# Value products of three attentions: two exponentials subtracted before one product, and fp16 pairs in place of fp32

## The reference, cut to what matters

```
# first block, 4 heads of width 128, each with two softmaxes over all keys (and 16 meta keys)
attn = softmax(q1 k1' * scale + bias) - lam * softmax(q2 k2' * scale + bias);   y = attn @ v
# (beside it a windowed attention, 8 heads of width 64, which the change leaves alone)
# second block, layer 0: 8 heads of width 64, dense and causal
y = softmax(causal(q k' * scale)) @ v
# second block, layer 1: 16 heads in 4 groups; per head three parts, each with a gate
y = g0 * softmax(q kc') @ vc + g1 * softmax(q ks') @ vs + g2 * softmax(q kw') @ vw
```

## Time and profile before

| what | us |
|---|---|
| median of 3 runs | 2100.46 (2099.26 to 2101.49) |
| the profiled execution | 2099.9 |
| its span, first to last instruction | 2098.1 |
| TensorE busy | 2036.8 (97%) |
| VectorE busy | 1185.9 (57%) |
| ScalarE busy | 809.9 (39%) |
| GpSimd busy | 38.5 (2%) |

### The profile page before, as it was taken

The page is one execution under the profiler, slowest core; times in us unless marked ns, Lnnn a source line. Parts: engine busy times, 40 slices in busy tenths (PEclk is TensorE's granted clock), DMA queues, the critical chain, the costliest instruction groups (busy, mean ns, idle before and its releaser), DMA issues. The chain is left out here.

```text
span 2098.1 us, 27744 instructions
## 1 busy us (share of the span) xinstructions
PE 2036.8 (97%) x10806; PEld 971.0 (46%) x10806; DVE 1185.9 (57%) x2179; ACT 809.9 (39%) x1476; POOL 38.5 (2%) x40
## 2 busy tenths in 40 slices
PE   9989999999999999989999999999999999999997
PEld 4444444444444444444444444447544444444443
DVE  6966744546554347776676623267766636864222
ACT  4447733323332232346333322235377733432220
POOL 2000000000000002000000000000000000000000
PEclk9999999999999999999999999997999999999998
DMA  6300233324333322312243333317100131433311
GB/s 218 97 1 1 71 93 105 97 74 125 100 101 121 101 71 90 102 51 81 61 121 105 100 109 105 104 39 232 35 1 1 31 92 40 147 104 109 102 41 40
DMA packets 53193, 179.19 MB, mean 85 GB/s; under 512 B 6096, under 2 KB 9808, under 8 KB 52816
## 3 DMA queue, kind: packets, MB, share of 16 engines
q1 hardware_dynamic: 53072, 177.51, 27.7%
HBM read 174.34 MB, written 2.10 MB: 84 GB/s over the span
## 5 line engine op out<-in xcount | busy, mean ns | idle before, releaser
L1748 DVE SCALAR_TENSOR_TENSOR w_lo<-w_raw,w_hi 128x1024 f16<-128x1024 f32 x317 | 385.3, 1219 | 167.3 <-ACT w_hi L1404 154.7
L1404 ACT ACTIVATE w_hi<-w_raw 128x1024 f16<-128x1024 f32 x317 | 330.7, 1048 | 269.9 <-PE pS L944 261.9
L942 PE MATMUL pS<-xx,w_hi 128*128 128x512 f16 x928 | 353.0, 380 | 1.4 <-DVE xx L1763 1.4
L943 PE MATMUL pS<-xx,w_hi 128*128 128x512 f16 x928 | 353.2, 381 | 0.0
L944 PE MATMUL pS<-xx,w_lo 128*128 128x512 f16 x928 | 353.1, 381 | 0.0
L942 PE MATMUL pS<-arena,w_hi 128*128 128x512 f16 x918 | 347.9, 379 | 2.1 <-DVE arena L1763 1.5
L944 PE MATMUL pS<-arena,w_lo 128*128 128x512 f16 x918 | 347.9, 379 | 0.0
L943 PE MATMUL pS<-arena,w_hi 128*128 128x512 f16 x918 | 347.9, 379 | 0.0
L1413 ACT ACTIVATE arena<-src 128x512 f16<-128x512 f32 x106 | 66.7, 630 | 321.3 <-DVE src L2399 164.0
L1819 DVE TENSOR_TENSOR tmp<-pS,rs 128x512 f32<-128x512 f32 x98 | 67.5, 688 | 138.0 <-PE pS L944 138.0
L944 PEld LDWEIGHTS pS<-xx,w_lo 128*128 128x128 f16 x928 | 91.0, 98 | 110.3 <-issue 1.4
(11 more groups left out here) (342 smaller groups left out, 2737.0 us busy)
## 6 DMA issues: line engine op xcount, KB each, us to landing
w_raw<-in_w SPq DMA_DIRECT2D x317, 512.0 KB, 3.6
X<-in_x SPq DMA_DIRECT2D x8, 264.0 KB, 6.7
arena<-in_c SPq DMA_DIRECT2D x2, 1024.0 KB, 5.6
out_t<-X SPq DMA_DIRECT2D x8, 256.0 KB, 2.0
arena<-in_h SPq DMA_DIRECT2D x4, 256.0 KB, 12.3
arena<-in_h SPq DMA_DIRECT2D x2, 512.0 KB, 9.4
arena<-in_c SPq DMA_DIRECT2D x2, 256.0 KB, 2.9
arena<-arena SPq DMA_DIRECT2D x4, 128.0 KB, 2.5
```

Source lines behind the costliest of these rows:

```text
L942: pe.matmul(ps, wh, ah, start=f, stop=False)
L943: pe.matmul(ps, wh, al, start=False, stop=False)
L1404: act.activation(w_hi[:, u % WR, :], w_raw[:, u % RAW, :], ACT.Copy, scale=WS).then_inc(hi_split, 1)
L1748: dve.scalar_tensor_tensor(out=w_lo[:, u % WR, :], in0=w_raw[:, u % RAW, :], scalar=WS, in1=w_hi[:, u % WR, :], op0=ALU.mult, op1=ALU.subt ...
```

## The change

* `diff` becomes paired like the others: units alternate between the two halves. After both exponentials of a pair VectorE computes `a - lam' b` into the first one's buffer (`combine`, one scalar_tensor_tensor), and TensorE makes one fp32 product with the unscaled values. The second copy of the values goes. TensorE waits at a tile's first slot for the rows of both halves.
* In `mla` and `nsa` each key unit gets two activations, both with a bias ln(2^14) from a tile `p_shift`: one in fp32 into `tmp`, one in fp16. GpSimd subtracts the second from the first and writes the fp16 lower part (`low_parts`). The values are evicted as two fp16 parts. The value product is three fp16 matmuls (high x high, low x high, high x low) in place of one in fp32; the output's eviction divides by 2^14.
* `key_exped` is incremented after the second activation, and TensorE's value products wait for GpSimd's `unit_low`.

```diff
@@ Run.number
-        if group[0].paired:
-            ...
-        else:
-            order = [(t, i) for t in group for i in range(t.n_units)]
-            self.values += [[u + x] for x in range(len(order))]
+        b, keys = len(group) // 2, len(group[0].keys)
+        order = [(group[x + h * b], i) for x in range(b) for i in range(keys) for h in range(2)]
+        pairs = [[u + x, u + x + 1] for x in range(0, len(order), 2)]
+        order += [(group[-1], keys)] * group[-1].extra
+        self.values += pairs + [[u + len(order) - 1]] * group[-1].extra
+        if group[0].joint:
+            self.joint += pairs
@@ gpsimd
+            def low_parts(run):
+                for u in range(run.u0, run.u1):
+                    t, i = UNITS[u]
+                    n = T if i == len(t.keys) else t.keys[i][-1][1] + t.keys[i][-1][3]
+                    h, l = exps(t, u)
+                    pool.wait_ge(key_exped, u + 1)
+                    pool.tensor_tensor(l[:, 0:n], tmp[:, u % 4, 0:n], h[:, 0:n], ALU.subtract).then_inc(unit_low, 1)
@@ tensor, unit_values
+                if t.split:
+                    pe.wait_ge(unit_low, us[-1] + 1 - RUNS["mla"].u0)
+                    for x, (v, p) in enumerate(((0, 0), (1, 0), (0, 1))):
+                        if i == len(t.keys):
+                            mm = pe.matmul(o, extra_values(t, v), exps(t, us[0])[p], start=False, stop=False, skip_group_check=True)
+                            ...
+                        for n_, (kb, c0, q0, n) in enumerate(t.keys[i]):
+                            for u in us:
+                                ...
+                                mm = pe.matmul(o[head_rows(t.half), q0:q0 + n], values(t, kb, v), exps(t, u)[p][:, c0:c0 + n], start=new,
+                                               stop=False, skip_group_check=True)
+                    ...
+                    return
                 pe.wait_ge(key_exped, us[-1] + 1)
+                if t.joint:
+                    (kb, _, _, _), = t.keys[i]
+                    pe.wait_ge(combined, JOINT[us[0]] + 1)
+                    pe.matmul(o, values(t, kb), tmp[:, us[0] % 4, :], start=i == 0, stop=False).then_inc(unit_av, 2)
+                    return
@@ tensor, attention
                     if t is not None and t.first:
-                        pe.wait_ge(lse_rows, t.lse + 1 + t.paired)
-                    elif t is not None and not t.paired:
-                        pe.wait_ge(lse_rows, t.lse + 1)
+                        pe.wait_ge(lse_rows, t.lse + 2)
@@ scalar, key_exp
-                act.activation(tmp[:, u % 4, 0:a.shape[1]], a, ACT.Exp).then_inc(key_exped, 1)
+                p = tmp[:, u % 4, 0:a.shape[1]]
+                if t.split:
+                    act.activation(p, a, ACT.Exp, bias=p_shift[:, :])
+                    act.activation(exps(t, u)[0][:, 0:a.shape[1]], a, ACT.Exp, bias=p_shift[:, :]).then_inc(key_exped, 1)
+                else:
+                    act.activation(p, a, ACT.Exp).then_inc(key_exped, 1)
@@ vector, value_m (value_c and the compressed values alike)
                 for half in range(2):
-                    ins = dve.tensor_scalar(vzm[:, t, :, 2 * half * HD:(2 * half + 1) * HD], ps[:, :, half, :], rnk[:, t:t + 1], None,
-                                            ALU.mult)
+                    link(dve.tensor_scalar(vh[half], ps[:, :, half, :], rnk[:, t:t + 1], None, ALU.mult))
+                sync()
+                for half in range(2):
+                    ins = dve.scalar_tensor_tensor(out=vl[half], in0=ps[:, :, half, :], scalar=rnk[:, t:t + 1], in1=vh[half],
+                                                   op0=ALU.mult, op1=ALU.subtract)
@@ vector, value_a
-                evict_N(S["va"], t, vd[:, 0, t, :], T, rn[:, t:t + 1])
-                moved(S["va"], t)
-                link(dve.tensor_scalar(vd[:, 1, t, :], vd[:, 0, t, :], nlam[:, :], None, ALU.mult))
+                evict_N(S["va"], t, vd[:, t, :], T, rn[:, t:t + 1])
@@ vector, attention: called in the step of the first unit behind a pair
+            def combine(us):
+                dve.wait_ge(key_exped, us[1] + 1)
+                a, b = (tmp[:, u % 4, :] for u in us)
+                dve.scalar_tensor_tensor(out=a, in0=b, scalar=nlam[:, :], in1=a, op0=ALU.mult, op1=ALU.add).then_inc(combined, 1)
+                        if now and joint and joint[0][1] < now[0].u[now[1]]:
+                            combine(joint.pop(0))
```

More of the change, by code:

```diff
@@ L291, in number @@
     def number(self, group, u):
[L293 to L301 removed]
+        b, keys = len(group) // 2, len(group[0].keys)
[5 more added lines that the diff above has]
+            self.joint += pairs
         for n, (t, i) in enumerate(order):
             t.u.append(u + n)
[L304 removed]
+            self.todo[min(n * len(group) // (len(order) - group[-1].extra), len(group) - 1) + group[0].s].append((t, i))
         for t in group:
@@ L658, in build_program @@
         MLA_END = at
-        vz, at = view(0, [NQ, 2, 6 * HD])
+        vz0, at = pair(0, [NQ, 2, 6 * HD])
+        vz = [v for v in vz0]
         q1h, at = view(at, [2 * N_YC, T], F16)
@@ L676, in build_program, with exps, values @@
         m_att, _ = view(6080, [8, T])
-        def values(t, kb):
+        def exps(t, u):
+            return [a[:, u % 4, :] for a in ((pm_hi, pm_lo) if t.kind.name == "mla" else (pn_hi, pn_lo))]
+        def values(t, kb, q=0):
             if t.kind.name == "diff":
-                return vd[:, t.half, kb, t.j * P:(t.j + 1) * P]
+                return vd[:, kb, t.j * P:(t.j + 1) * P]
             a = 2 * t.half * HD
@@ L1165, in unit_values @@
                         t = UNITS[u][0]
-                        rows = head_rows(t.half) if t.paired else slice(0, P)
-                        new = t.b == 0 and i == 0 and n_ == 0 and (t.paired or t.first)
+                        rows = head_rows(t.half)
+                        new = t.b == 0 and i == 0 and n_ == 0
                         mm = pe.matmul(o[rows, q0:q0 + n], values(t, kb), tmp[:, u % 4, c0:c0 + n], start=new, stop=False,
-                                       skip_group_check=t.paired)
+                                       skip_group_check=True)
                         if n_ == len(t.keys[i]) - 1:
@@ L2111, in value_c @@
                 ps = out_of(S["vv"], t).rearrange("p (c d) -> p c d", d=2 * HD)
+                vh, vl = ([v[:, t, :, :].rearrange("p b (g d) -> p (b g) d", g=2)[:, :, 2 * HD * half:2 * HD * half + HD]
+                           for half in range(2)] for v in vz)
+                pv = [ps[:, :, HD * half:HD * (half + 1)] for half in range(2)]
                 for half in range(2):
-                    to = vz[:, t, :, :].rearrange("p b (g d) -> p (b g) d", g=2)[:, :, 2 * HD * half:2 * HD * half + HD]
-                    ins = dve.tensor_scalar(to, ps[:, :, HD * half:HD * (half + 1)], rn[:, t:t + 1], None, ALU.mult)
+                    link(dve.tensor_scalar(vh[half], pv[half], rn[:, t:t + 1], None, ALU.mult))
+                sync()
+                for half in range(2):
+                    ins = dve.scalar_tensor_tensor(out=vl[half], in0=pv[half], scalar=rn[:, t:t + 1], in1=vh[half], op0=ALU.mult,
+                                                   op1=ALU.subtract)
                     if half == 0:
@@ L2172, in _ @@
             dve.memset(ones[:, :], 1.0)
+            dve.memset(p_shift[:, :], float(np.log(PS)))
             dve.memset(half_neg[:, :], -0.5).then_inc(basics_ready, 1)
```

70 lines of the change are left out of this document (47 added, 23 removed).

## The result

The changed kernel takes 2177.43 us (median of 4 runs, 2174.48 to 2181.9) against 2100.18: a ratio of 1.0367, 95% interval 1.0355 to 1.0379. The direction was forecast; the size was not, 2144 having been named and 2174 as the range's end. The profiled execution took 2174.48, its span is 2172.7, so 74.6 us more than before.

A forecast was written before the change was run, and what follows sets the result against it. TensorE, busy 97%, was taken to bound the kernel, with ScalarE setting the pace in the changed second and third runs. -8 + 35 + 10 + 3.5 + 1.5 + 1.8 = +43.8 us gave 2144 us, range 2116 to 2174.

The forecast's parts named there:

- The third run, +35: Third attention run: a second, biased exponential per key unit makes ScalarE set the pace, adding 35 us.
- I add 1.2 us for each of eight tiles and 1.7 for the end: Third run: allowance for ScalarE's stalls and the final series of steps, taking its +24 us to +35.
- a floor of 178 us: Third run: ScalarE's work, 182.6 us less some 5 us of overlapped tails, as the least time, +24 us.
- The first attention, -8: First attention: 16 fewer value products on TensorE against VectorE's combinations, 8 us gained, bounds 13.8 and 0.
- so I take 15.2 us a period: First attention: tile period falls from 17.17 to 15.2 us, with three engines within 12% of each other.
- The small terms: Second run +10 us; splitting values ahead of second run +3.5, ahead of third +1.5; compressed values' second halves +1.8.
- The clock: Rival, second and third run: TensorE idles a quarter of the time and its clock falls; 2154 to 2170, chance 0.10.
- the port conflict: Rival, third run: GpSimd and VectorE hold each other up, +12 to +25 us, 2156 to 2169; chance 0.15.
- GpSimd as the bound: Rival, third run: subtractions above 2.2 us per 512 columns set the pace; 2216 at 3 us, chance 0.02.
- The packed case: Rival: ScalarE packs without stalls and the first attention gives its whole 13.8 us; 2121, chance 0.14.
- The faster case: Rival: the second exponential fits in ScalarE's idle time, so TensorE's savings count; 2079, chance 0.04.
- The step for ScalarE: Second and third run: two biased activations per key unit add 14.2 and 62.3 us of ScalarE work.

The follow-up runs named there:

- warm: The changed kernel with one unread 512-column matmul ahead of each key unit's scores in the second and third run; 2172.46 us.
- no_pool_no_shift: The changed kernel without GpSimd's subtractions (third product takes the upper part again) and with both exponentials without the bias tile and factor 2^14; 2137.85 us.
- one_exp: The changed kernel without GpSimd's subtractions and without the fp32 exponential, only the fp16 one per unit; lower parts left out; 2102.27 us.
- no_pool: The changed kernel without GpSimd's subtractions; the third product takes the upper part again and products wait for the exponential; 2169.86 us.
- no_shift: The changed kernel with both exponentials without the tile as bias and so without the factor 2^14; 2168.86 us.
- dve_high: The changed kernel with one fp32 exponential per unit on ScalarE, VectorE copying it as fp16 a step later, GpSimd still subtracting; 2202.84 us.
- no_pool_warm: The changed kernel without GpSimd's subtractions and with one unread 512-column matmul ahead of each split key unit's scores; 2165.05 us.

## Why the prediction was right or wrong

**The third run, +35, was mis-sized: +53.** The step that failed is "I add 1.2 us for each of eight tiles and 1.7 for the end". ScalarE's work itself was right: a floor of 178 us was forecast and it is busy for 179.69. What was sized too small is the time in which it stands idle: some 10 us were allowed in the run (153.2 + 35 less 178), and it has 28.3. The first part of the step held where the clock was full (24.5 forecast, 24.7 measured, ScalarE 93% busy), and so did the start of the run up to its first compressed unit (+4.0) and its end behind the last (+1.9). Against 24.5 and the shape of before, the excess of the seven periods is 17.0 us:
* 0.2 + 1.1 + 2.6 + 2.7 + 2.7 = 9.3 in the five full tiles, from the second on together with the granted clock at 0.50. `warm` shows the cause for the most part: with the clock at 1.00 all five are 25.15, 6.0 us less together, its own matmuls counted in. The forecast took the 77% of the earlier trace rows at clock 1.00 as evidence against a fall, but that stretch was 24 us long, while here the first tile too stayed at 1.00 with 76%, and the falls came 70 us into the run.
* 4.0 + 3.7 = 7.7 in the last two periods. They grew by 8.3 and 8.0 us, and ScalarE's busy time in them by 7.6 and 7.8, where a full tile grew by 4.5 at full clock with 7.1 more work. A mean of 4.3 a tile overlooked that here ScalarE's idle time took up none of it. Part of why is GpSimd: without it they are 25.2 and 19.0. The 2.4 of the last tile are its own (at clock 1.00 in `warm` that tile is still 21.1); of the 1.5 in the one before, the clock may have a share, as it is 25.2 in `warm` too.

**The first attention, -8, was wrong: 0.** The bound of 0 stood in the text ("if each of the 16 waits for the combination costs TensorE what the product gave back"), with waits of up to 1.0 us that is what happened. The step that failed is "so I take 15.2 us a period"; it took engine loads per period, not the order on VectorE, where the combination comes behind a maximum that waits for later scores.

**The small terms were right in place and nearly in size.** Ahead of the second run +3.7 (3.5), second run +10.7 (10), TensorE's wait of 4.2 us at 6.2 (6.0). After the second run a stretch of 6.8 us at half clock came as a surprise; TensorE was busy 4.98 us of it, so it cost at most 2.5 us. Of the +4.2 between the runs 2.0 are the wait's, and 2.2 lie ahead of the wait, which this stretch can account for. Ahead of the third run the conversion of the values cost 2.2 (1.5, with a bound of 3.8).

**The rivals.** The clock and the port conflict both came true, but as exclusive cases with 0.25 between them they couldn't widen the sum; the range ended 3 us under the time. The port conflict was priced at +12 to +25 and cost nothing that can be told here, and 13.5 without the pointer. GpSimd as the bound is excluded: 13.07 of 24.70 us busy. But the forecast had its latency hidden as long as a subtraction stays below some 2.5 us, and at 1.16 us TensorE already waits 19.2 us for it in the third run, and it cost 7.6 of the whole. The packed case fell: even in a full-clock tile of `no_pool_no_shift`, 22.7 us, some 2 us of ScalarE are idle. The faster case is excluded by `one_exp`, 2102 with none of the second exponentials and none of GpSimd's work. The step for ScalarE carried the sign, and the runs bear it out: the second exponentials cost 67.6 us. As work they are the forecast's 62.3 + 14.2 less the pointer of the first ones (0.09 x 128 = 11.5), 65.0. That the two agree is luck: idle time took up a part of this work in the full tiles, and stalls and falls of the clock added about as much.

Left open is why the falls begin at 1629.5 here, at 1594 in `no_pool`, whose tiles are equally busy, and at 1571 in `no_shift`.

## What to carry to other kernels

When several limits lie within a tenth of each other (here ScalarE's load, its pointer operands, GpSimd's turn, the clock), removing one shows only the gap to the next: GpSimd was worth 7.6 us beside the pointer and 31.0 without it. Price a design with all removed, and each added back, before trusting a single-removal number. And for work inserted in a fixed order of waits, look at which instruction stands ahead of it and what that one waits for, before looking at the engine's load.

## What the runs showed of the hardware

* A GpSimd subtraction of fp32 less fp16 to fp16 takes 1158 to 1175 ns for 128x512 and 670 for 128x256. The Trainium skill, GPSIMD Engine Reference, section 3.1, gave the estimate of 1.11 us for the first; the trace is 4 to 6% above.
* Beside it VectorE's additions and multiplications on twelve SBUF columns grow from 160 to 180 ns to as much as 1.1 us, while casts of twelve columns keep their 206. Its fp16 copies of 128x512 take 0.42 us where no subtraction overlaps them and up to 1.27 where one does (`dve_high`; mean 548 ns).
* The granted clock fell to 0.50 in a stage with TensorE 76% busy, again and again, 70 us after the stage began, and not in the five full tiles of `warm` (83% busy in the one shown), where the first fall behind the run's start is at 1731. But it fell in two full tiles of `no_pool_warm`, whose first tile is 84% busy (21.18 of 25.10 us).
* Three fp16 passes of a pair's 512-column unit, start to start, take 0.78 us at full clock, where the fp32 product took 1.01.
